# One expert row more in eight fetched in halves, whole rows summed one by one, and a third pair of PSUM banks for the sums

## The reference, cut to what matters

```
x = x + peer_ffn(rms_norm_2(x, ln_ffn_g), w_query, sub_keys, expert_u, expert_v)

def block(xb):                       # 128 tokens at a time, 4 blocks
    q  = (xb @ w_query).reshape(128, 8, 2, 128)
    sc = einsum('thpd,hpkd->thpk', q, sub_keys)
    s_top, i_top = top_k(sc, 16)
    cand = s_top[:, :, 0, :, None] + s_top[:, :, 1, None, :]
    best, pos = top_k(cand.reshape(128, 8, 256), 16)
    eidx = take_along_axis(i_top[..0..] * 128 + i_top[..1..], pos)
    g  = softmax(best)
    h  = gelu(einsum('thkd,td->thk', expert_u[eidx], xb))
    return einsum('thk,thkd->td', g * h, expert_v[eidx])
```

## Time and profile before

| | |
|---|---|
| median of three runs | 3165.66 us |
| the profiled execution, its own time | 3168.34 us |
| its span | 3166.5 us |
| PE, DVE, ACT, POOL busy | 2533.9, 1588.9, 1025.8, 723.9 us |
| gathers of `peer_uv` | 674 |
| bytes of POOL's queue | 508.16 MB |

### The profile page before, as it was taken

One profiled execution on the slowest core, in us unless ns is written; L12 is line 12 of the kernel. 1 busy time (PEld: TensorE's weight loads), 2 busy tenths in 40 slices (PEclk: granted clock), 3 DMA queues, 4 the chain that ended last, 5 costly groups with the idle time before them and its releaser, 6 DMA issues.

```text
span 3166.5 us, 44150 instructions
## 1 busy us (share of the span) xinstructions
PE 2533.9 (80%) x17242; PEld 1262.3 (40%) x17242; DVE 1588.9 (50%) x3644; ACT 1025.8 (32%) x2341; POOL 723.9 (23%) x697
## 2 busy tenths in 40 slices
PE   8999987798988888888878888798867756666665
PEld 6677765385332222222226744353424311111111
DVE  4656655763100100100105466667676678788774
ACT  2533443511000000000004445468543334344343
POOL 0000000000000000000000043333455666666663
PEclk9999998898999999999999998888878877778777
DMA  4311302157999999999996399999999999999998
GB/s 151 105 59 67 124 26 114 54 200 323 427 427 427 426 427 427 426 427 427 428 427 237 115 412 399 419 418 398 400 404 389 363 392 412 413 412 407 412 413 314
DMA packets 152000, 1032.78 MB, mean 326 GB/s; under 512 B 25445, under 2 KB 28389, under 8 KB 71664
## 3 DMA queue, kind: packets, MB, share of 16 engines
q1 hardware_dynamic: 53008, 521.81, 40.1%
q0 software_dynamic: 98784, 508.16, 39.8%
HBM read 1051.58 MB, written 13.37 MB: 336 GB/s over the span
## 4 chain that ended last, share of the span: by engine, by line
DMA 38%; PE 38%; DVE 9%; ACT 6%; issue 4%; POOL 4%; another core or an unknown queue 1%; ACTq 0%; DVEq 0%; SPq 0%; POOLq 0%
PE ps L96 20%; PE ps_pair L96 17%; DMA gb<-in_peer_uv,eidx 15%; DMA ga<-in_eu 8%; DMA gw<-in_eu 7%; DMA gw<-in_ed 5%; DMA ga<-in_ed 3%; DVE gb L150 3%; POOL gb L88 3%; ACT L172 1%; ACT dots L172 1%; PE ps L101 1%; POOL gb L90 1%; PE ps_pair L101 1%; ACT diag L172 1%
## 5 line engine op out<-in xcount | busy, mean ns | idle before, releaser
L88 POOL DMA_INDIRECT gb<-in_peer_uv,eidx x520 | 553.5, 1064 | 1083.6 <-DVE eidx L130 525.8
L96 PE MATMUL ps<-gb,diag 64*64 64x512 f32 x3136 | 494.0, 736 | 258.7 <-ACT diag L172 123.0
L150 DVE CUSTOM_DVE_ANT_0 gb<-gb,xn 128x1024 f32<-128x1024 f32 x256 | 312.7, 1221 | 171.4 <-DMA gb<-in_peer_uv,eidx 162.0
L150 DVE CUSTOM_DVE_ANT_0 gb<-gb,ps_pair 128x1024 f32<-128x1024 f32 x256 | 311.5, 1217 | 128.0 <-DMA gb<-in_peer_uv,eidx 81.5
L96 PEld LDWEIGHTS ps<-gb,diag 64*64 64x64 f32 x3136 | 117.6, 155 | 564.8 <-issue 252.1
L119 DVE TENSOR_TENSOR expert_act<-expert_act,ps_pair 128x512 f32<-128x512 f32 x32 | 22.0, 687 | 525.5 <-PE ps_pair L96 525.0
L96 PE MATMUL ps_pair<-ga,xt 128*64 128x512 f32 x1024 | 231.2, 599 | 41.9 <-DMA ga<-in_eu 34.4
L96 PE MATMUL ps_pair<-gb,diag 64*64 64x512 f32 x960 | 165.5, 819 | 103.3 <-DMA gb<-in_peer_uv,eidx 64.7
L96 PE MATMUL ps_pair<-gw,xt 128*64 128x512 f32 x992 | 225.0, 602 | 24.2 <-DMA gw<-in_eu 14.9
L172 ACT ACTIVATE diag<-cons,dots 128x128 f32<-128x128 f32 x512 | 205.6, 401 | 76.1 <-remote 27.7
L172 ACT ACTIVATE dots<-dots 128x1 f32<-128x1 f32 (+1 forms) x266 | 54.2, 204 | 498.4 <-DVE soft L130 196.2
(11 more groups left out here) (433 smaller groups left out, 4144.3 us busy)
## 6 DMA issues: line engine op xcount, KB each, us to landing
ga<-in_eu SPq DMA_DIRECT2D x47, 2048.0 KB, 35.5
gw<-in_eg SPq DMA_DIRECT2D x46, 2048.0 KB, 30.6
ring<-in_wt SPq DMA_DIRECT2D x75, 1024.0 KB, 5.6
gw<-in_ed SPq DMA_DIRECT2D x32, 2048.0 KB, 35.5
ga<-in_ed SPq DMA_DIRECT2D x32, 2048.0 KB, 36.0
ga<-in_eg SPq DMA_DIRECT2D x17, 2048.0 KB, 32.7
gw<-in_eu SPq DMA_DIRECT2D x16, 2048.0 KB, 35.5
gb<-in_peer_uv,eidx POOLq DMA_INDIRECT x674, 13.8
```

What stands on the lines that cost most here:

```text
L88: self.e.indirect_dma_start(out, None, table, at).then_inc(s, 16)
L96: i = self.e.matmul(out, l, r, start=st, stop=sp, skip_group_check=True)
L150: self.done(self.e.tensor_tensor_reduce(out=o, in0=a, in1=b, scale=scale, scalar=start, op0=o0, op1=o1, accum_out=acc), name)
```

## The change

- `whole(n)`: rows 176 to 255 as before (four of eight split). From 256 to 495 the rows with n % 8 in 0, 2, 4 are whole and 1, 3, 5, 6, 7 split, so that quads have two and three split rows by turns; 256 and 384 are whole now. That makes 190 split rows, 182 of them gated.
- The order of the sums is the order of the gathers that bring v: a whole row's gelu, weight, diagonal and sum stand right behind its own dot, and a v half's behind the u parts of the quad two further on. Gelu is done by itself for each whole row and together for the two or three (four before) of a quad that are split; so are mask and index. Sums of two tiles may alternate now.
- Tile 2 adds up in banks 2 and 3, no longer in 6 and 7, and starts without waiting for tile 1's end. Its tokens stay in banks 0 and 1. The tokens of tile 3 are put into banks 6 and 7 by ScalarE (two copies of 128x512) at row 288, once tile 1 is finished.
- The indices are doubled for all of a head in rows 256 to 495 and halved again for its whole rows; in 176 to 255 those of the split rows are doubled.

```diff
-    VBS = [[6, 7], [6, 7], [6, 7], [0, 1]]
+    VBS = [[6, 7], [6, 7], [2, 3], [0, 1]]
+    TOKENS = [XN[0], XN[1], XP[0], XP[2]]
...
     def whole(n):
-        return n < HALVED or n % 4 in (0, 2) and n % 128 != 0 or n >= WHOLE
+        if n < MORE:
+            return n < HALVED or n % 4 != 1 or 120 <= n < 128
+        return n % 8 in (0, 2, 4) + (6,) * (n < 256) or n >= WHOLE
...
-    def sums_after(n):
-        if n < HALVED:
-            return list(row_group(n)) if n == row_group(n)[-1] else []
-        if n >= LAST:
-            k = n - LAST
-            return [[500, 501], [502, 503], [504, 505], [506, 507]][k] if k < 4 else [n]
-        g, j = n // 4, n % 4
-        before = [m for m in quad(g - 1) if whole(m)] if g > HALVED // 4 else []
-        later = [m for m in quad(g - 2) if not whole(m)] if g > HALVED // 4 + 1 else []
-        todo = later + before if g % 32 == 1 or g > WHOLE // 4 else before + later
-        return todo[j * len(todo) // 4:(j + 1) * len(todo) // 4]
-    SUMS = [m for n in range(512) for m in sums_after(n)]
+    def split_of(g):
+        return [n for n in quad(g) if not whole(n)]
+    GATHERS = [("u", n) for n in range(HALVED + 4 * LEAD)]
+    for g in range(HALVED // 4, WHOLE // 4):
+        GATHERS += [("u", n) for n in quad(g + LEAD)] + [("v", n) for n in split_of(g)]
+    GATHERS += [("u", n) for n in range(WHOLE + 4 * LEAD, 512)]
+    SUMS = [n for e, n in GATHERS if e == "v" or whole(n)]
...
+        for kind, n in GATHERS:
+            if kind == "v":
+                yield from summed(n)
+                continue
...
             yield ("u", n)
-            if n == group[-1]:
-                yield ("k", group)
-            for m in sums_after(n):
-                yield ("w", m)
...
+            if whole(n):
+                yield ("k", (n,))
+                yield from summed(n)
+            if n % 4 == 3 and split_of(n // 4):
+                yield ("k", tuple(split_of(n // 4)))
...
+            if n == 288:
+                yield ("tokens",)
...
-                if at % 128 == 0:
-                    pe.wait_ge(*left if i == 0 else [("dot", 383) if i == 3 else ("rows_end", i - 1)])
+                if n == ROW_STARTS[i]:
+                    pe.wait_ge(*left if i == 0 else [[("rows_end", 0)], [("xn3g", 3)], [("dot", 383)]][i - 1])
...
-                ac.wait_ge(("mask", n // 4) if HALVED <= n < WHOLE else ("dot", n))
+                ac.wait_ge(("dot", n) if whole(n) else ("mask", n // 4))
...
+            elif ev[0] == "tokens":
+                ac.wait_ge(("xn3g", 3), ("rows_end", 1))
+                for half in range(2):
+                    q = slice(512 * half, 512 * half + 512)
+                    ac.act(XP[2][:, q], XN[3][:, q], ACT.Copy, name="tokens")
...
-            dv.ts(w_, w_, 0.5, MUL, name=("eidx", i, h))
+            dv.ts(w_, w_, 0.5 if most else 2.0, MUL, name=("eidx", i, h))
...
-                dv.ttr(u, u, XN[i] if i < 2 else XP[i - 2], 1.0, 0.0, MUL, ADD, dots[:, i % 2, k:k + 1], name=("dot", n), free=True)
+                dv.ttr(u, u, TOKENS[i], 1.0, 0.0, MUL, ADD, dots[:, i % 2, k:k + 1], name=("dot", n), free=True)
```

More of the change, by code:

```diff
@@ L215, in block_program @@
     PS = [XP[i // 2][:, 512 * (i % 2):512 * (i % 2) + 512] for i in range(4)]
-    PS += [nc.alloc_psum_tensor(f"ps{i}", [128, 512], F32)[:, :] for i in range(4, 8)]
+    PS += [nc.alloc_psum_tensor(f"ps{i}", [128, 512], F32)[:, :] for i in (4, 5)]
+    XP.append(nc.alloc_psum_tensor("ps_pair2", [128, 1024], F32)[:, :])
+    PS += [XP[2][:, 512 * i:512 * i + 512] for i in range(2)]
     p_dram = nc.dram_tensor("p_scratch", (128, 35 * 512), F32, kind="Internal").ap()
@@ L3021, in ac_peer @@
                 ac.wait_ge(("inv", i, k // 16))
-                if HALVED <= n < WHOLE:
+                if not whole(n):
                     ac.wait_ge(("mask", n // 4))
@@ L3050, in dv_choose @@
             yield
-        if 8 * i + h < HALVED // 16:
+        most = 256 <= 128 * i + 16 * h < WHOLE
+        if most:
+            dv.ts(sif, siu, 2.0, MUL)
+        else:
             dv.cp(sif, siu)
-        else:
-            dv.ts(sif, siu, 2.0, MUL)
         yield
@@ L3086, in dv_choose @@
         dv.stt(eidx[i % 2][:, 16 * h:16 * h + 16], e12[:, 0, :], 128.0, e12[:, 1, :], MUL, ADD, name=("eidx", i, h))
-        if 8 * i + h >= HALVED // 16:
+        cut = [n % 16 for n in range(128 * i + 16 * h, 128 * i + 16 * h + 16) if not whole(n)]
+        if cut:
             w_ = eidx[i % 2][:, 16 * h:16 * h + 16]
-            if (i, h) != (3, 7):
-                w_ = w_[:, 0 if h else 2:16:2]
+            if most:
+                w_ = w_.rearrange("p (a b) -> p a b", b=8)[:, :, 0:5:2]
+            else:
+                w_ = w_[:, cut[0]:cut[-1] + 1:cut[1] - cut[0]]
             was, dv.link = dv.link, None if dv.link is None else dv.n
-            dv.ts(w_, w_, 0.5, MUL, name=("eidx", i, h))
+            dv.ts(w_, w_, 0.5 if most else 2.0, MUL, name=("eidx", i, h))
             dv.link = was
@@ L3173, in v_row @@
             po.gather(v_of(n), halves, eidx[i % 2][:, k:k + 1], f"gv{s}", ("v_row", n), 2 * 16384 - 1 if gated(n // 4) else None)
-        for n in range(HALVED + 4 * LEAD):
-            u_row(n)
-        for g in range(HALVED // 4, WHOLE // 4):
-            for n in quad(g + LEAD):
+        for kind, n in GATHERS:
+            if kind == "u":
                 u_row(n)
-            for n in quad(g):
-                if not whole(n):
-                    v_row(n)
-        for n in range(WHOLE + 4 * LEAD, 512):
-            u_row(n)
+            else:
+                v_row(n)
     def pe_program(pe):
```

59 lines of the change are left out of this document (28 added, 31 removed).

## The result

3211.3 us (median of four runs, 3197.7 to 3230.1) against 3165.0 of the kernel before beside it: ratio 1.0149, interval 1.0129 to 1.0169. Slower, where 3135 was forecast. The profiled execution took 3197.7 us (span 3195.2).

A forecast was written before the change was run, and what follows sets the result against it. The prediction took DMA, full at 412 GB/s from 2625 to 2875 us, as the bound. Its terms, 13 + 14 + 0.7 + 2 + 1.5 = 31 us, took 3168.3 to 3137, given as 3135 for the median; range 3127 to 3145.

The forecast's parts named there:

- What is added beside this: Extra ACT, PE and v-half work over the split rows: hidden by DMA, v halves' cover 17.7 us for 18.2, cost 0.
- Term 1: Rows 256 to 495: 28 more split rows save skipped bytes, 13 us (11.7 to 15.3).
- Term 2: Before row 272: POOL's waits for sums shrink, regaining 14 of 20.3 us lost (0 to 20).
- No POOL wait over 5 us: Sign for Term 2: none between 2400 and 2600 us, with 400 GB/s or more there.
- Term 3: Tile 3's start: POOL's 7.30 us wait goes, gaining 0.7 us.
- Term 4: The tail, 3100 to 3150 us and the end: 2 us from POOL's waits, 1.5 us from PE's end.
- PE's end: Part of Term 4: no sums put off to rows 504 to 507, some 1.5 us less (0 to 2).
- I am wrong if DMA's share in the middle of rows 272 to 480 falls: Sign against the whole forecast; DMA's share was 1.02 in the full stretch before the change.
- Rival C: Rows 256 to 495: POOL becomes the bound, 19.2 us for eight rows against 18.35; slower, 3181 us; chance 0.08.
- Gathers of 1.1 us and more behind row 256: Sign for Rival C, together with DMA's share under 0.98.
- Rival A: Only the bytes gain: waits return behind the projections or as waits for v halves; 13 + 2 us, 3151; chance 0.17.

The follow-up runs named there:

- e11: The changed kernel, text for text, run again in a set where results were on time: 3139.8 us, ratio 0.993.
- e3: The changed kernel with five places for whole rows and eight for pairs of halves, in place of six and seven: 3141.4 us, ratio 0.9931.
- e8: The changed kernel, unchanged, run again in a set where results were late: 3219.5 us, ratio 1.0182.
- e9: e3 with the places of rows 496 to 508 taken in the order in which they come free, results late: 3181.3 us, ratio 1.0058.
- e7: The changed kernel with the gelu of a quad's split rows moved behind the v sums of two quads before, results late: 3196.6 us, ratio 1.0098.
- e12: The changed kernel with four rows of eight split from row 176 to 495, results on time: 3156.9 us, ratio 0.9978.
- set 1: Four variants run beside the kernel before on chip 5, results on time: 3155.6, 3146.8, 3141.4 and 3180.7 us.
- e2: The kernel before, in its own order and banks, with five of eight rows split between 256 and 495, results on time: 3146.8 us, ratio 0.9958.
- e5: The changed kernel, unchanged, run again in a set where results were late: 3217.9 us, ratio 1.0166.
- e6: The kernel before, unchanged, run for a profile in a set where results were late: 3161.8 us, ratio 0.9993.
- The tail's line: Places of rows 496 to 508 are taken as they come free, not by row number; added alone to the changed kernel, results late: 3206.0 us.
- e16: The changed kernel with four of eight split and rows 496 to 508 taking places as they come free, results late: 3147.3 us, ratio 0.994.
- e10: e2 with five places for whole rows and eight for pairs of halves, results late: 3203.1 us, ratio 1.0126.
- e15: The changed kernel with the tokens of rows 256 to 511 read from SBUF, in a late set: 3185.9 us, ratio 1.0067.

## Why the prediction was wrong

The step that failed stands at the end of "What is added beside this": "V halves: ... 17.7 us, for 18.2 now. That is the new tightest cover; 0." It counts the cover in front of a v half's index. The cover behind its place is not counted there, and what is added on ACT is called "hidden by DMA". In the changed order seven places serve five of eight rows, and from a v half's gather to the one that takes its place lie 7.2 to 10.2 rows' worth of transfers, counted with 43% of v halves skipped, where it was 10.2 to 13.7. At 2.5 us a row that is 18 us for 25. What it must cover: in e11 a v half's sum is done 5.3 us after its landing, and a gather lands some 13 us after its issue. 5.3 + 13 is 18. On time it just fits: in e11 the tightest places are filled again 0.8 us after their sum, where in e3, with eight places, some 6 us lie between. With results late by 5 us and more it no longer fits, and DMA runs dry; and ACT, which stands on a late score, holds the diagonals of the sums back too. The runs size these parts only roughly. Rows 272 to 480 take 534.1 us in e8 and 468.4 in e11; eight places give 25 of these 66 us back (e9), and one event moved in ACT's order 25 in its own set (e7). The rest is not accounted for.

Point by point, first where results are on time (e11):

- *Term 1, bytes, 13 us.* Right. POOL's queue moved 501.62 MB for 508.16, 6.54 less (6.3 forecast), with 702 gathers. Rows 272 to 480 took 468.4 us for 479.0: 10.6 us for 25 of the 28 rows, 0.42 each, at the lower bound. Against four of eight in the same set (e12, 26 rows fewer) it is 12.4 us, 0.48 each.
- *Term 2, 14 us.* Right where results are on time: rows 176 to 272 take 234.9 us in e11, for 254.9 and 248.0 in the two traces of the kernel before, both late; and in set 1 234.6 in e3 for 247.5 in e2, which has the order before. Not steady where they are late: 236.3 for 254.9 in the first traces, but 242.8 in e5 for 248.0 in e6 beside it, so 5 to 19 us. "No POOL wait over 5 us" is wrong: three v halves wait 5.8 to 6.5 us there in the first trace, and two 6.3 us in e11, but DMA stays full behind them.
- *Term 3.* Right: no wait near tile 3's start, 408 GB/s in 2875 to 2900.
- *Term 4, 3.5 us.* Wrong in sign for the tail: rows 480 to 511 take 84.2 us for 80.8. POOL's waits there in e11:

```profile
3074.52 0.94 POOL L88 DMA_INDIRECT gb<-in_peer_uv,eidx  x1 [10.96 <-PE ps_pair L96]
...
3088.24 0.94 POOL L88 DMA_INDIRECT gb<-in_peer_uv,eidx  x1 [7.67 <-PE ps_pair L96]
...
3103.84 0.94 POOL L88 DMA_INDIRECT gb<-in_peer_uv,eidx  x1 [7.01 <-PE ps_pair L96]
```

 11.0 us for row 499's place is more than the 8.4 that went. I had let 499 stand "as close behind its v half as now"; its place comes free with the sum of row 486's v half, which the new order puts behind the whole rows of two quads later, while the places of rows 488 and 490 lay free. The tail's line takes 6 to 9 us of it back (78.1 for 87.4, 80.4 for 86.7). PE's end was right: from the last dot to the end of the span 9.2 us for 10.6, in e11 and in the first trace, and sums of 1.93 us with pauses between, as in the first trace's last three:

```profile
3183.38 1.93 PE L96 MATMUL ps<-gb,diag 64*64 64x512 f32 x8 [0.55 <-ACT diag L172]
3185.89 1.93 PE L96 MATMUL ps<-gb,diag 64*64 64x512 f32 x8 [0.57 <-ACT diag L172]
3188.36 1.93 PE L96 MATMUL ps<-gb,diag 64*64 64x512 f32 x8 [0.54 <-ACT diag L172]
```

Their sum, 3139.8 for 3135, lies inside the forecast's own range. Then what no term held:

- *Late results.* Shown: the same program loses 44 to 60 us in rows 272 to 480 where they are late, nothing where they are on time. The kernel before bears them, as e16 does. That the late results cause the loss, and not something that brings both, rests on the waits in the traces. "I am wrong if DMA's share in the middle of rows 272 to 480 falls" is what happened; the sign on which to see it coming was in the trace: score copies that waited 16.1 us in all, up to 3.9 at once, behind matmuls that had ended.
- *Rival C* gave the right sign, not the cause. Gathers of 1.1 us and more behind row 256 were not seen in the changed kernel (962 and 996 ns). As a mechanism it is real: with the tokens in SBUF gathers take 1226 and 1176 ns and rows 272 to 480 take 504 us:

```profile
L88 POOL DMA_INDIRECT gb<-in_peer_uv,eidx x103 | 126.3, 1226 | 31.4 <-issue 26.2 <-PE ps_pair L96 2.7 <-DVE cand L119 1.2
L90 POOL DMA_INDIRECT gb<-in_peer_uv,eidx x64 | 75.3, 1176 | 19.5 <-issue 15.8 <-DVE pos L124 1.8 <-DVE top_s L158 0.6
```

 13 x (1.21 + 0.3) = 19.6 us for eight rows by C's own sum; 504.4 / 26 = 19.4 measured. It cost 39 us (3178.5 for 3139.8). By this the split of five rows stands on the tokens' being in PSUM, and with them there most of the late results come.
- *Rival A's* second half, "waits for v halves, whose sums now stand in front of whole rows in one queue", named the place. It was priced at the bytes alone, 3151.

Not settled: why results are late in some sets and not in others. Nor what the new order and the new banks have to do with it: the score copies of the changed kernel wait 72 to 115 us in 2600 to 3050 us, those of the kernel before 16 and 23 and of e10, which has its order and banks, 15; no run changes the order without the banks. Semaphore events are missing from the late traces (577 to 609 updates of PE's counter from 1800 us on, for 639 in each on-time one), so that the recording may have a part in it; every time here comes from recorded executions. Nor why e9 still loses with places as far apart as e16's. That POOL needs 16.6 us of 17.9 for eight rows with five split, 15.3 of 18.3 with four, and so catches up on a wait more slowly, would fit; it is only argued, from the forecast's own sums.

Best so far: the changed kernel where results are on time (0.993). Over both kinds e16, the new order with four of eight split and the tail's line: 0.994 where results are late, and without that line 0.998 where they are on time.

## What to carry to other kernels

Count the cover of every place, from the gather that fills it to the one that reuses it, and set it against landing to release plus issue to landing; a place that just covers both was full in one set of runs and dry in the next. An engine that works in one order passes a late result on to everything behind its consumer. Before trusting a cover, look in the trace for consumers that start long after their producer's record has ended: that delay is part of the cover. A change that removes slack is worth measuring in several sets; 0.993 and 1.018 were the same program.

## What was unexpected of the hardware

- TensorE's results can come up to 14 us after the matmul's record ends (e8), in some sets of runs and not in others on the same chip, mostly while VectorE's dots read PSUM. The kernel before shows it too, and its medians beside all sets lie within 0.15% (3161.9 to 3166.4 us).
- VectorE's dot takes the same time with tokens from PSUM (1214 ns) as from SBUF (1221 ns), but GpSimd's gathers beside it take 0.96 and 1.00 us with PSUM (e11) and 1.23 and 1.18 with SBUF (e15). For five of eight split rows that is 36 us of the kernel.
